# Moving norm-modulation units of a fused two-block transformer kernel to other weight products

## The reference

```
h = layer_norm(a*h + stick_breaking(h @ sb_win) @ mix_wo)
h = layer_norm(a*h + cross_attention(h @ xa_wq, mem @ xa_wkv) @ xa_wo)
x = layer_norm(a*h + (gelu(g) * val) @ ffn_down)        # g, val = conv3(h @ ffn_up)
cs = silu(c)
for i in range(2):
    sh_m, sc_m, g_m, sh_f, sc_f, g_f = split(cs @ mod_w[i] + mod_b[i], 6)
    if i == 1: shared k, v from adaln(x, kv_norm, *split(cs @ kv_mod_w + kv_mod_b, 2))
    y = mamba2(adaln(x, ..., sh_m, sc_m)) if i == 0 else nsa(adaln(x, ..., sh_m, sc_m), shared)
    x = x + g_m * rmsnorm(y)
    x = x + g_f * rmsnorm((silu(a) * b) @ ffn_w_out)    # a, b = adaln(x, ..., sh_f, sc_f) @ ffn_w_in
```

## Time and profile before

| | |
|---|---|
| median of 3 runs | 2856.29 us (2851.35 to 2857.38) |
| the profiled execution: its time, its span | 2854.78 us, 2853.1 us |
| PE busy | 2600.0 us (91%) |
| DVE busy | 1352.4 us (47%) |
| ACT busy | 1072.4 us (38%) |
| POOL busy | 206.3 us (7%) |
| granted clock of PE, mean over the span | 0.965 |
| waits of PE for a modulation unit (L888 for L2110) | 23.9 us, 11 times |

### The profile page before, as it was taken

How to read it: one execution, slowest core, us unless ns; L and a number is a source line. 1 busy time by engine, 2 the same in 40 slices (tenths; PEclk the granted TensorE clock), 3 DMA queues, 4 the chain that set the end, 5 groups by cost and what they waited for, 6 DMA issues and landing times.

```text
span 2853.1 us, 35119 instructions
## 1 busy us (share of the span) xinstructions
PE 2600.0 (91%) x13316; PEld 2107.0 (74%) x13316; DVE 1352.4 (47%) x1869; ACT 1072.4 (38%) x1569; POOL 206.3 (7%) x249
## 2 busy tenths in 40 slices
PE   6978789788999988988899999999997888999999
PEld 5855578567887877776468888888875666788887
DVE  5764377567764355423554333235525544433323
ACT  2235422223454134434644333234424554433322
POOL 1101111001000010000201000001001111100000
PEclk8989989899999999999999999999989999999999
DMA  7730174424323222221012222323310000223232
GB/s 247 265 117 1 47 249 147 162 73 163 118 89 110 96 62 74 88 74 59 1 38 89 89 90 93 103 89 105 104 55 15 22 15 7 67 90 102 90 100 83
DMA packets 178691, 263.21 MB, mean 92 GB/s; under 512 B 8232, under 2 KB 127904, under 8 KB 178592
## 3 DMA queue, kind: packets, MB, share of 16 engines
q1 hardware_dynamic: 156608, 194.00, 20.9%
q0 software_dynamic: 15232, 58.72, 5.9%
q10 hardware_dynamic: 6752, 9.09, 0.9%
HBM read 255.51 MB, written 2.10 MB: 90 GB/s over the span
## 4 chain that ended last, share of the span: by engine, by line
PE 72%; DVE 12%; ACT 7%; issue 5%; POOL 3%; DMA 1%; DVEq 0%; ACTq 0%; SPq 0%; POOLq 0%
PE ps L689 20%; PE ps L691 19%; PE ps L690 19%; PE ps L1281 2%; DVE wlo L2087 2%; PE ps L916 2%; ACT decay L1875 1%; PE ps L958 1%; DVE macc L2104 1%; PE ps L1386 1%; ACT pnt_h L1986 1%; DVE pnt_l L2091 1%; DVE nst L2608 1%; POOL diag L2867 1%; PE ps L1201 1%
## 5 line engine op out<-in xcount | busy, mean ns | idle before, releaser
L2087 DVE TENSOR_TENSOR wlo<-raw,whi 128x2048 fp32r<-128x2048 f32 x180 | 412.1, 2290 | 729.2 <-ACT whi L1506 729.0
L689 PE MATMUL ps<-acth,wlo 128*128 128x512 f32 (+1 forms) x1888 | 703.4, 373 | 24.1 <-DVE actl L2091 12.6
L691 PE MATMUL ps<-acth,whi 128*128 128x512 f32 (+1 forms) x1888 | 696.6, 369 | 0.0
L690 PE MATMUL ps<-actl,whi 128*128 128x512 f32 (+1 forms) x1888 | 696.5, 369 | 0.0
L1506 ACT ACTIVATE whi<-raw 128x2048 fp32r<-128x2048 f32 x180 | 343.6, 1910 | 585.5 <-PE ps L691 585.5
L689 PEld LDWEIGHTS ps<-acth,wlo 128*128 128x128 f32 x1888 | 358.1, 190 | 87.9 <-DVE actl L2091 15.1
L690 PEld LDWEIGHTS ps<-actl,whi 128*128 128x128 f32 x1888 | 358.1, 190 | 60.1 <-issue 1.2
L691 PEld LDWEIGHTS ps<-acth,whi 128*128 128x128 f32 x1888 | 357.4, 189 | 59.8
L689 PE MATMUL ps<-whi,hid_l 128*128 128x512 f32 x528 | 207.9, 394 | 5.2 <-DVE conv_t L2315 3.4
L690 PE MATMUL ps<-wlo,hid_h 128*128 128x512 f32 x528 | 206.2, 390 | 0.0
L691 PE MATMUL ps<-whi,hid_h 128*128 128x512 f32 x528 | 206.0, 390 | 0.0
(11 more groups left out here) (329 smaller groups left out, 3690.9 us busy)
## 6 DMA issues: line engine op xcount, KB each, us to landing
mraw<-in_mod_w POOLq DMA_DIRECT2D x48, 1024.0 KB, 5.5
raw<-in_ffn_w_in SPq DMA_DIRECT2D x44, 1024.0 KB, 4.9
raw<-in_ffn_up SPq DMA_DIRECT2D x22, 1024.0 KB, 4.9
raw<-in_ssm_w_in SPq DMA_DIRECT2D x20, 1024.0 KB, 5.1
raw<-in_ffn_w_out SPq DMA_DIRECT2D x20, 1024.0 KB, 4.9
raw<-in_sb_win SPq DMA_DIRECT2D x12, 1024.0 KB, 5.0
raw<-in_ffn_down SPq DMA_DIRECT2D x10, 1024.0 KB, 4.9
raw<-in_xa_wkv SPq DMA_DIRECT2D x8, 1024.0 KB, 5.1
```

The lines of the kernel that those rows point to most:

```text
L689: nc.tensor.matmul(o, ll, rh, start=start, stop=False, skip_group_check=True)
L690: nc.tensor.matmul(o, lh, rl, start=False, stop=False, skip_group_check=True)
L691: return nc.tensor.matmul(o, lh, rh, start=False, stop=stop, skip_group_check=True)
L2087: nc.vector.tensor_tensor(wlo[:, slot, :], raw[:, slot, :], whi[:, slot, :].bitcast(F32), ALU.subtract) \
```

## The change

The units are dealt out anew. The memory product and the first pairs of `xa_wq` and of the convolution feed-forward take none. The token products of `mix_wo` and `xa_wo` and the second pair of `xa_wq` keep four each. In the convolution feed-forward the pairs 1 to 6 take two each (before: 0 to 3), and one of the two is done by DVE at the head of the turn, ahead of the taps. The eight units for the shared keys and values go to the pairs 1 to 4 of the first gated feed-forward, two each, at the head of DVE's turn; their gain row is computed there too. POOL's loads are put in the same order. The number of units, their instructions and their loads stay.

```diff
-        def gated_ffn(turn=None):
+        def gated_ffn(turn=None, mods=0):
...
+            def gated_pairs(pairs, mods):
+
+                with turns.loop(pe, pairs, {unit_ready: 2, hid_value: 2, mod_acc: mods}):
...
+                    if mods:
+                        mod_columns(mods)
+                mods_behind[0] += pairs if mods else 0
+
             first_turn(branch_out, scaled, value_free)
...
+            if mods:
+                gated_pairs(4, mods)
+            gated_pairs(FC // 2 - 1 - (4 if mods else 0), 0)
...
-        feature_pairs(2, memh, meml, MEM, mods=2)
-        token_pairs(2, memh, meml, nt=MB, mods=2)
+        feature_pairs(2, memh, meml, MEM)
+        token_pairs(2, memh, meml, nt=MB)
 
         banks_out()
         token_product(acth, actl, KC, h_sum, summed, mods=4)
-        first_pair(h_sum, summed, mods=4)
+        first_pair(h_sum, summed)
         feature_pairs(1, acth, actl, mods=4)
         cross_attention()
         banks_out()
         token_product(acth, actl, KC, h_sum, summed, mods=4)
-        first_pair(h_sum, summed, conv_done, mods=2)
-        feature_pairs(3, acth, actl, free=conv_done, mods=2, out=False)
-        feature_pairs(FC // 2 - 4, acth, actl, free=conv_done)
+        first_pair(h_sum, summed, conv_done)
+        feature_pairs(6, acth, actl, free=conv_done, mods=2, out=False)
+        feature_pairs(FC // 2 - 7, acth, actl, free=conv_done)
...
-        gated_ffn(scaled)
+        gated_ffn(scaled, mods=2)
...
         def conv_ffn():
-            conv_pairs_of_ffn(4, 0, 2)
-            conv_pairs_of_ffn(FC // 2 - 4, 4, 0)
+            conv_pairs_of_ffn(1, 0, 0)
+            conv_pairs_of_ffn(6, 1, 2)
+            conv_pairs_of_ffn(FC // 2 - 7, 7, 0)
...
                 turns(marks, 4)
+                mod_units(0, mods // 2)
                 for u in range(2):
...
                     if u == 0:
                         split(0)
-                        mod_units(0, mods)
+                        mod_units(mods // 2, mods - mods // 2)
...
+        def gated_pairs(pairs, first, mods):
+
+            with turns.loop(dve, pairs, {hi_ready: 2, gated: 2, evac_hi: 2, marks: 4} | mod_steps(mods)) as turn:
+                i = turn + first if first else turn
+                mod_units(0, mods)
                 split(0)
...
         pool.wait_ge(o_free, 2 + KC)
-        mod_loads(2, 2, a["mod_w_2"][1], 0)
-        mod_loads(2, 2, a["mod_w_2"][1], 4)
+        mod_loads(1, 4, a["mod_w_2"][1], 0)
+        block_roots(sum_block, False)
+        mod_loads(1, 4, a["mod_w_2"][1], 4)
         mod_loads(1, 4, a["mod_w_2"][1], 8)
         block_roots(sum_block, False)
-        mod_loads(2, 4, a["mod_w_2"][1], 12)
-        mod_loads(1, 4, a["mod_w_2"][1], 20)
-        block_roots(sum_block, False)
-        mod_loads(4, 2, a["kv_mod_w_2"], 0)
+        mod_loads(6, 2, a["mod_w_2"][1], 12)
...
         block_roots(branch_block, True)
+        mod_loads(4, 2, a["kv_mod_w_2"], 0)
         block_roots(branch_block, True)
```

More of the change, by code:

```diff
@@ L2333, in conv_pairs_of_ffn @@
                 if mods:
-                    mod_store(mods, 2 * mods * i + 96)
+                    mod_store(mods, 2 * mods * turn + 72)
         def stored(ins, done=dve_step):
@@ L2390, in branch_norm @@
                 low_block(3)
-        def gated_ffn(gate, low_block=None):
-            with turns.loop(dve, FC // 2, {hi_ready: 2, gated: 2, evac_hi: 2, marks: 4}) as i:
+        def gated_pairs(pairs, first, mods):
+            with turns.loop(dve, pairs, {hi_ready: 2, gated: 2, evac_hi: 2, marks: 4} | mod_steps(mods)) as turn:
+                i = turn + first if first else turn
+                mod_units(0, mods)
                 split(0)
@@ L2405, in gated_ffn @@
                     lo_part(hid_l[:, 2 * i + j, :], conv_t[:, j, :], hid_h[:, 2 * i + j, :]).then_inc(hid_ready, 1)
+                if mods:
+                    mod_store(mods, 2 * mods * turn + 96)
+        def gated_ffn(gate, low_block=None, mods=0):
+            if mods:
+                gated_pairs(1, 0, 0)
+                gated_pairs(4, 1, mods)
+                dve.wait_ge(mod_done, 19)
+                gain_columns(4, 104, C_KVN)
+                gated_pairs(FC // 2 - 5, 5, 0)
+            else:
+                gated_pairs(FC // 2, 0, 0)
             branch_norm(gate, FC, by_block(branch_t), low_block)
@@ L2672, in _, with gain_columns @@
         turned_los(meml, memh, MB)
[L2673 to L2675 removed]
+        splits(2)
+        token_banks(2, lambda i, t: nc.vector.tensor_copy(vx[:, t, bass.ds(512 * i, 512)], ps[:, t, :]), nt=MB)
         summed = lambda t: turned_lo_block(actl, acth, t)
         scaled = lambda gain, shift: lambda t: modulated_lo_block(actl, acth, t, gain, shift)
+        residual_norm(summed, mods=4, col=48)
+        splits(1)
+        splits(1, mods=4, col=56)
+        cross_attention()
         residual_norm(summed, mods=4, col=64)
[L2679 to L2681 removed]
         conv_ffn()
[L2684 to L2686 removed]
+        def gain_columns(n, scale, g):
             nc.vector.scalar_tensor_tensor(out=gains[:, n, :], in0=modv[:, scale:scale + KC], scalar=1.0,
                                            in1=cols[:, g:g + KC], op0=ALU.add, op1=ALU.mult)
+        dve.wait_ge(mod_done, 15)
+        for n, (scale, g) in enumerate(((8, C_PRE_MIX), (56, C_PRE_MIX + KC), (32, C_PRE_FFN), (80, C_PRE_FFN + KC))):
+            gain_columns(n, scale, g)
         residual_norm(scaled(0, 0), FC)
```

36 lines of the change are left out of this document (13 added, 23 removed).

## The result

The changed kernel took 2825.43 us in the median of 4 runs (2816.64 to 2827.59), beside 2856.43 us (4 runs, 2851.35 to 2857.38) for the kernel before: ratio 0.9894, 95% interval 0.9873 to 0.9915. The forecast was 2817.5 us with a range of 2809 to 2832. The direction and the range held, and so did the likeliest case, in which no rival comes true; 7.9 us of the gain are missing by the medians. The two profiled executions are further apart from the forecast: their spans differ by 27.2 us (2853.1 and 2825.9), 11.6 less than the 38.8 forecast.

The account below looks back on a forecast made before the run. PE's waits for units' last additions (23.9 us) and slower clock behind them bound the kernel; 18.8 + 10.7 + 12.7 - 3.4 = 38.8 us off 2854.8 gives 2816.0, plus 1.5 to the median: 2817.5 us, range 2809 to 2832.

Parts of the forecast that it names:

- the likeliest case: Whole kernel: the forecast sum holds and no rival comes true, 2817.5 us, own range 2811 to 2824; chance 0.66.
- Memory product: Without units, 64.5 us from the first pair's end to the end of `mix_wo`'s first unit become 45.7: gain 18.8 us.
- `xa_wq`: Its two pairs: without units in the first, 17.0 us to the second pair's first bank become 6.3: gain 10.7 us.
- Convolution feed-forward: To the end of pair 6, 148.4 us become six pairs at 22.61, 135.7 us: gain 12.7 us if no pair waits.
- Gated feed-forward: First gated feed-forward: eight units of columns at 0.43 us each cost 3.4 us; DVE's work fits its free stretch.
- The slack on DVE: Convolution feed-forward pairs: the second unit ends at 815.3, PE's pair at 817, about 2 us of slack.
- rival C: Convolution feed-forward: six pairs still wait, 1.35 us each, 2825.6 us, with half clock up to 2836; chance 0.15.
- one stretch of half clock above: Upper end of the forecast's own range, 2824 us: bank waits of 2.0 us each and one half-clock stretch elsewhere.
- The clock term: Of the 38.8 us gain, 12.5 come from windows behind PE's waits in the changed stages returning to full clock.
- B: Waits go but the clock stays down, as short bank-copy waits might lower it: gain 26.3 us, 2830 us; chance 0.12.
- D: Late unit loads hold up DVE, then PE, in ten pairs: slower than before, 2905.5 or 2925.5 us; chance 0.03.
- E: No change: the units' 24 us of waiting come up elsewhere, as DVE owes the same work: 2856 us; chance 0.04.

## Why the prediction came out as it did

**What bounded it** was read rightly: PE's waits for the last addition of a unit, and a slower product behind them. All 23.9 us of them went.

**Memory product**: gain 18.8 predicted, 18.2 found; the two new waits are 0.3 us longer than taken. **`xa_wq`**: 10.7 and 10.4. Put back, the two pairs cost 12.2 us (longer waits, 4.18 and 3.45 us, and more half clock), of which the cross attention behind them, untouched, gave back 1.6 against the second and third profiles. **Convolution feed-forward**: 12.7 and 12.1 (six pairs at 22.7 instead of 22.6; two units' columns cost 0.95, not 0.85). **Gated feed-forward**: cost 3.4 and 3.8, for the same reason. Together 36.9 of 38.8.

**The slack on DVE** was 1.75 us where "about 2" was predicted (817 - 815.3 = 1.7 by its own figures), and is made by the order: with both units behind the split rival C came true at its own price.

**The step that fell short** is in the sum: "18.8 + 10.7 + 12.7 - 3.4 = 38.8 us", taken as the gain of the whole. It supposes that all stages behind move ahead unchanged. In the first pair of profiles they lost 5.7 us behind 1803.75 and 1.5 us between 906.64 and 1060.03, and about 2 us lie ahead of 566. The first loss stands in all three profiles of the change (5.7 to 6.2 us against any of before), because work that comes at another time meets the changes of the clock elsewhere. The two small ones aren't repeated: the second profile of the change took 151.8 us from the first to the second of these waits, where before took 153.4 and the first profile of the change 154.9. The forecast's own range (2811 to 2824) allowed "one stretch of half clock above" for it, which was too little; the wide range held it. That the late loss is of this kind was shown by moving the work, once; for the two small ones it is only argued.

**The clock term** of 12.5 us was right for the profile it was read from, and came back in full in the stages changed. It was no fixed price: in the third profile of before the memory product lost 3.4 us less to the clock behind the same waits. The rest of 2.4 us, which the prediction calls the higher price of columns that come one by one, is what remains after the 2.3 us of new waits that its sums already charge; that price is 4.7 us by its own figures.

**The rivals.** B (the clock doesn't come back) is out: the waits of 0.77 to 0.97 us had no half clock behind them. D (late loads) is out: in the changed kernel DVE never waits for `mraw`, and the units' loads landed as before:

```profile
DMA to landing us min/median/max: 5.3/5.6/12.5
```

By its example for the "DVE blocks DMA" trap, a copy on DVE that uses both ports, the Trainium skill ("SBUF — State Buffer") would give landings of some 28 us, an estimate. Here none was over 12.5, with DVE at work in half of the span; which of its instructions use both ports the traces don't say.

The kernel before did have late loads, which the prediction didn't read: DVE waits there for `mraw` 5 times, 9.5 us in all, 8.2 of them in the two pairs of `xa_wq` (timeline of DVE):

```profile
487.99 0.62 DVE L2107 TENSOR_SCALAR macc<-mraw,c_silu 128x256 f32<-128x256 f32 x2 [2.90 <-DMA mraw<-in_mod_w]
493.63 0.62 DVE L2107 TENSOR_SCALAR macc<-mraw,c_silu 128x256 f32<-128x256 f32 x2 [2.19 <-DMA mraw<-in_mod_w]
```

POOL issues the first of these loads only at 481.90, behind the roots of the norm. Without the load waits the last unit behind which PE stands would have been done some 2.7 us earlier, an estimate from these rows; so PE's 6.9 us of waiting there came in part from late loads, not from DVE's order alone. With the first pair's units put back, DVE waited for `mraw` 8.1 us again.

E (the waits come up elsewhere) is out: PE's list of waits shows no new row of more than 1 us.

## What to carry to other kernels

Owed work that an engine does in order belongs where that engine stands waiting for others: count its free stretch per turn and put one piece ahead of it, one behind; the order alone gave 9.8 us here and its loss cost 16 to 19. See also that the loads for it are issued in time. A wait of PE may cost its own length again in clock, but that part is to be carried as a range. When work moves in time, add some 5 us either way for the places where later stages meet half clock (with the units behind the split one untouched part was 8 us longer), and compare where both traces stand at common waits, not spans alone: that tells what a stage gave from what was lost behind it.

## What the runs showed of the hardware

- Half clock isn't drawn afresh in each execution: three profiles of before, and three of the change, had their long stretches of the sparse attention at the same places against the work, within 0.5 us. Yet a shift of 2.95 us changed 14 + 10.5 us of half clock there into 7.
- The same four waits of 1.86 to 2.00 us in the memory product were followed by some 17 us of half clock in three profiles (two of the kernel before, and the order alone) and by 7 us in two others (the third of before, and the memory product's units put back). Waits of 1.16 to 1.32 us in the convolution feed-forward were followed by it in 2 of 6 pairs with the units behind the split and in 1 of 9 in the three profiles of before; the new waits of 0.77 to 0.97 us in none.
- Eight dummy matmuls in a wait of 1.86 us kept the next pair at full clock (11.6 instead of 13.1 us) and delayed nothing.
